# Moving the compressed branch and four out-branch tiles in a fused three-block transformer kernel

## What is computed

```python
blocks = t[:, :, cmp_idx] + pos_emb                    # 15 windows of 32 tokens, keys and values
k_cmp = rms_norm(jax.nn.gelu(flat_k @ w1[0]) @ w2[0], k_gain[0])
v_cmp = jax.nn.gelu(flat_v @ w1[1]) @ w2[1]
sc = jnp.einsum('bgrqd,bgcd->bgrqc', qb, k_cmp) * SCALE
pc = masked_softmax(sc, cmp_end[None, :] <= t[:, None])
o_cmp = jnp.einsum('bgrqc,bgcd->bgrqd', pc, v_cmp)
...
o = gates[0] * o_cmp + gates[1] * o_slc + gates[2] * o_win
y = (o * jax.nn.silu(z)) @ w_out
```

## Time and profile before

| | us |
|---|---|
| runs of the kernel before, median of 3 | 863.43 (860.35 to 863.61) |
| the profiled execution's own time | 864.82 |
| its span, first to last instruction | 863.0 |
| TensorE busy in the span | 810.6 (94%) |
| VectorE busy | 551.3 (64%) |
| ScalarE busy | 420.1 (49%) |
| mean granted TensorE clock | 0.982 of full |

### The profile page before, as it was taken

One profiled execution on the slowest core, in us unless ns is written; L12 is line 12 of the kernel. 1 busy time (PEld: TensorE's weight loads), 2 busy tenths in 40 slices (PEclk: granted clock), 3 DMA queues, 4 the chain that ended last, 5 costly groups with the idle time before them and its releaser, 6 DMA issues.

```text
span 863.0 us, 13766 instructions
## 1 busy us (share of the span) xinstructions
PE 810.6 (94%) x5402; PEld 716.2 (83%) x5402; DVE 551.3 (64%) x930; ACT 420.1 (49%) x820; POOL 114.0 (13%) x114
## 2 busy tenths in 40 slices
PE   4989798998979899999999999998999999999997
PEld 3768797776869687999988988888997788999995
DVE  5897667846796946345635657676675646555555
ACT  5434636844646634446436445553444434444443
POOL 2334004521522402000000000011000000000000
PEclk9989899999999999999999999998999999999999
DMA  8746310213533234553532433333544646655541
GB/s 310 205 155 196 99 49 2 98 68 117 185 104 126 71 123 146 165 178 126 166 101 89 157 118 127 99 114 119 183 154 140 198 144 223 203 187 194 189 154 49
DMA packets 93504, 121.42 MB, mean 141 GB/s; under 512 B 8760, under 2 KB 69616, under 8 KB 93440
## 3 DMA queue, kind: packets, MB, share of 16 engines
q1 hardware_dynamic: 92432, 117.80, 42.1%
q0 software_dynamic: 432, 1.57, 0.5%
q10 hardware_dynamic: 576, 1.17, 0.4%
HBM read 119.48 MB, written 1.05 MB: 140 GB/s over the span
## 4 chain that ended last, share of the span: by engine, by line
PE 77%; DVE 13%; issue 3%; ACT 2%; POOL 1%; POOLq 0%; DVEq 0%; ACTq 0%
PE bank L411 21%; PE bank L413 21%; PE bank L412 21%; DVE w_lo L1443 3%; PE bank L547 1%; DVE small L1534 1%; PE bank L603 1%; PE bank L919 1%; PE bank L418 1%; PE bank L417 1%; PE bank L561 1%; PE bank L541 1%; DVE h_lo L1568 1%; DVE xres L1646 1%; PE bank L859 1%
## 5 line engine op out<-in xcount | busy, mean ns | idle before, releaser
L1443 DVE TENSOR_TENSOR w_lo<-raw,w_hi 128x1024 fp32r<-128x1024 f32 x216 | 268.4, 1248 | 142.3 <-ACT w_hi L1053 140.2
L1053 ACT CAST w_hi<-raw 128x1024 fp32r<-128x1024 f32 (+1 forms) x217 | 226.0, 1045 | 201.0 <-PE bank L413 179.2
L411 PE MATMUL bank<-h_hi,w_hi 128*128 128x256 f32 (+1 forms) x800 | 230.4, 288 | 4.0 <-DVE w_lo L1443 2.9
L412 PE MATMUL bank<-h_lo,w_hi 128*128 128x256 f32 (+1 forms) x800 | 227.3, 284 | 0.0
L413 PE MATMUL bank<-h_hi,w_lo 128*128 128x256 f32 (+1 forms) x800 | 226.4, 283 | 0.0
L411 PEld LDWEIGHTS bank<-h_hi,w_hi 128*128 128x128 f32 x800 | 151.3, 189 | 9.5 <-issue 6.7
L413 PEld LDWEIGHTS bank<-h_hi,w_lo 128*128 128x128 f32 x800 | 152.1, 190 | 0.0
L412 PEld LDWEIGHTS bank<-h_lo,w_hi 128*128 128x128 f32 x800 | 151.7, 190 | 0.4
L411 PE MATMUL bank<-w_hi,h_hi 128*128 128x512 f32 (+1 forms) x288 | 115.8, 402 | 11.9 <-DVE w_lo L1443 6.2
L413 PE MATMUL bank<-w_hi,h_lo 128*128 128x512 f32 (+1 forms) x288 | 113.0, 392 | 0.0
L412 PE MATMUL bank<-w_lo,h_hi 128*128 128x512 f32 (+1 forms) x288 | 113.0, 392 | 0.0
(11 more groups left out here) (309 smaller groups left out, 1234.5 us busy)
## 6 DMA issues: line engine op xcount, KB each, us to landing
raw<-in_w_in SPq DMA_DIRECT2D x24, 1024.0 KB, 5.1
raw<-in_a_w_in SPq DMA_DIRECT2D x14, 1024.0 KB, 5.5
raw<-in_w_ffn_gate SPq DMA_DIRECT2D x11, 1024.0 KB, 5.3
raw<-in_w_ffn_up SPq DMA_DIRECT2D x11, 1024.0 KB, 5.4
raw<-in_w_ffn_down SPq DMA_DIRECT2D x11, 1024.0 KB, 4.9
raw<-in_b_w_in SPq DMA_DIRECT2D x9, 1024.0 KB, 5.2
raw<-in_w_gate SPq DMA_DIRECT2D x8, 1024.0 KB, 5.3
raw<-in_a_w_out SPq DMA_DIRECT2D x4, 1024.0 KB, 5.2
```

The costliest lines, as they stand in the source:

```text
L411: mm(o, lh, rh, start=start, stop=False)
L412: mm(o, lh, rl, start=False, stop=False)
L1053: nc.scalar.copy(split(w_hi, s), rawsub(s)[0]).then_inc(S["hi_ready"], 1)
L1443: V.tensor_tensor(split(w_lo, s), rawsub(s)[0], split(w_hi, s).bitcast(F), ALU.subtract).then_inc(S["lo_ready"], 1)
```

## The change

Five edits. In the first block, the transposes of the compressed inputs (0 to 3) go to banks 0 to 3 and stand between the panels `a_s` and `a_w`; ScalarE's copies of them follow its work on `a_s`; the query and key transposes are spread between the z tiles, and the compression matmuls follow z tile 0. The 32 score matmuls, four at a time, alternate with the eight steps of z tile 5. In the differential attention, branch tiles 0 to 3 of `br_sb` go into rounds 8 and 9, and VectorE's and ScalarE's order follows. The third output projection waits for six merged tiles, not eight, before its first half, and for all eight before its second. The sum of the two statistics goes from GpSimd to VectorE for the first token tile of each norm and for both tiles of the last norm.

```diff
--- before.py
+++ after.py
@@ -498,12 +498,10 @@
                 for e, src in enumerate(srcs, e0):
-                    if phase == 0 and 4 <= e < 8:
-                        pe.wait_ge(S["tq_c"], e - 3)
-                    elif e >= 4:
+                    if e >= (4 if phase else 8):
...
                     for j, t in enumerate(src):
-                        last = nc.tensor.transpose(tbank(e)[:, P * j:P * j + P], t, ident)
+                        last = nc.tensor.transpose((ps[e] if phase == 0 and e < 4 else tbank(e))[:, P * j:P * j + P], t, ident)
@@ -630,6 +628,8 @@
                         pe.wait_ge(S[ready], base + step * (q + 1))
+                    elif n == 3:
+                        pe.wait_ge(S["y_df"], 8)
@@ -669,9 +669,12 @@
             pe.wait_ge(S["rp_act"], 6)
+            pe.wait_ge(S["rp_c"], 2)
+            head_transposes(0, 0, k_tiles(0, 4) + k_tiles(1, 4))
...
             weights_ready(s)
+            pe.wait_ge(S["tq_c"], 4)
@@ -682,33 +685,27 @@
             za = first["a_z"]
+            pe.wait_ge(S["rp_free"], 8)
+            pe.wait_ge(S["rp_act"], 8)
+            pe.wait_ge(S["rp_out"], 4)
+            head_transposes(4, 0, q_tiles(0))
...
             o.then_inc(S["gl_ps"], 1)
-            z_tiles(0, za, 1, 2)
-            pe.wait_ge(S["rp_free"], 8)
-            pe.wait_ge(S["rp_act"], 8)
-            pe.wait_ge(S["rp_c"], 2)
-            head_transposes(0, 0, k_tiles(0, 4))
-            pe.wait_ge(S["rp_free"], 10)
-            pe.wait_ge(S["rp_out"], 4)
-            head_transposes(2, 0, k_tiles(1, 4) + q_tiles(0) + q_tiles(1))
-            pe.wait_ge(S["gates"], 1)
-            pe.wait_ge(S["tq_c"], 4)
...
             last.then_inc(S["cm_ps"], 1)
+            pe.wait_ge(S["rp_free"], 10)
+            head_transposes(6, 0, q_tiles(1))
+            z_tiles(0, za, 1, 2)
+            pe.wait_ge(S["rp_out"], 6)
+            head_transposes(8, 0, k_tiles(2, 4))
             z_tiles(0, za, 2, 3)
-            pe.wait_ge(S["rp_out"], 8)
-            head_transposes(8, 0, k_tiles(2, 4) + k_tiles(3, 4))
-            z_tiles(0, za, 3, 4)
@@ -716,16 +713,29 @@
             last.then_inc(S["cm_ps2"], 1)
-            z_tiles(0, za, 4, 5)
+            pe.wait_ge(S["rp_out"], 8)
+            head_transposes(10, 0, k_tiles(3, 4))
+            z_tiles(0, za, 3, 4)
...
             nc.tensor.transpose(ps[3][:, 256:320], kcd, ident[0:64, 0:64]).then_inc(S["cm_ps3"], 1)
-            z_tiles(0, za, 5, 6)
+            z_tiles(0, za, 4, 5)
             pe.wait_ge(S["cm_kt"], 1)
-            for qt in range(2):
-                for h in range(NH):
+            def compressed_scores(a, b):
+                for i in range(a, b):
+                    qt, h = divmod(i, NH)
...
                               kc[:, h // 4].rearrange("p i c -> p (i c)"), start=True, stop=True)
-            last.then_inc(S["cm_s"], 1)
+                return last
+            pe.wait_ge(S["z_free"], 4)
+            weights_ready(za + 5)
+            wh, wl = split(w_hi, za + 5), split(w_lo, za + 5)
+            for kt in range(KT):
+                last = three(ps[1][:, 0:T], wh[:, kt, :], wl[:, kt, :], tok(0, kt), tok(1, kt), kt == 0, kt == KT - 1)
+                scored = compressed_scores(4 * kt, 4 * kt + 4)
+            last.then_inc(S["sub_used"], 1)
+            scored.then_inc(S["cm_s"], 1)
@@ -942,6 +952,15 @@
+            def br_sb_tile(f):
+                if f < 2:
+                    pe.wait_ge(S["gt_t"], 15 + f)
+                elif f < 4:
+                    pe.wait_ge(S["d_p"], 13 + f)
+                else:
+                    pe.wait_ge(S["y_sb"], f - 3)
+                fm_tile(first["br_sb"] + f, om(o1_hi), om(o1_lo), ps[f % 4][:, 0:T])
@@ -951,11 +970,15 @@
                     pe.wait_ge(S["zb_olo"], 8)
+                if h >= 8:
+                    br_sb_tile(2 * h - 16)
...
                     gate_tile(2 * h + 1)
+                else:
+                    br_sb_tile(2 * h - 15)
@@ -968,12 +991,9 @@
-            pe.wait_ge(S["gt_t"], 16)
-            for f in range(8):
-                if f >= 4:
-                    pe.wait_ge(S["y_sb"], f - 3)
-                fm_tile(first["br_sb"] + f, om(o1_hi), om(o1_lo), ps[f % 4][:, 0:T])
-                if f == 4:
+            for f in range(4, 8):
+                br_sb_tile(f)
+                if f == 5:
@@ -982,7 +1002,7 @@
                 fm_tile(first["br_df"] + f, om(o2_hi), om(o2_lo), ps[f % 4][:, 0:T])
-            pe.wait_ge(S["y_df"], 8)
+            pe.wait_ge(S["y_df"], 6)
@@ -1098,7 +1118,7 @@
                 act.wait_ge(S["tq_ps"], e + 1)
-                b = tbank(e)[:, :].rearrange("p (g n) -> p g n", g=4)
+                b = ps[e][:, :].rearrange("p (g n) -> p g n", g=4)
@@ -1197,25 +1217,33 @@
                     head_item(first[n] + 4, b, 256, vv[j][:, i, :], ps[b][:, 256:512], 0, 4 + 2 * j + i)
+                if n == "a_s":
+                    for i in range(4):
+                        c_copy(i, i // 2, i % 2)
...
             za = first["a_z"]
-            split_hi_to(za + 5)
+            for i in range(2):
+                q_hi(4 + i, 0, 0, i)
+            split_hi_to(za + 4)
...
             A(sm[:, 48:144], sm[:, 48:144], ACT.Tanh, scale=0.5).then_inc(S["gl_t"], 1)
-            split_hi_to(za + 6)
-            z_tanh(0, za, 1)
-            for i in range(4):
-                c_copy(i, i // 2, i % 2)
-            for i in range(4):
-                q_hi(4 + i, 0, i // 2, i % 2)
+            split_hi_to(za + 5)
+            q_hi(6, 0, 1, 0)
...
             A(xg, xg, ACT.Tanh, scale=0.7978845608028654).then_inc(S["cm_t"], 1)
-            for i in range(4):
-                key_hi(8 + i, 0, i // 2, i % 2, 4)
-            for f in range(2, 6):
+            q_hi(7, 0, 1, 1)
+            z_tanh(0, za, 1)
+            split_hi_to(za + 6)
+            for i in range(2):
+                key_hi(8 + i, 0, 0, i, 4)
+            z_tanh(0, za, 2)
+            split_hi_to(za + 7)
+            for i in range(2):
+                key_hi(10 + i, 0, 1, i, 4)
+            for f in range(3, 6):
@@ -1371,8 +1399,8 @@
                     df_squares(h - 3)
-            split_hi_to(first["br_sb"] + RING - 1)
             for h in range(5, 8):
+                split_hi_to(first["br_sb"] + h - 5 + RING)
@@ -1452,9 +1480,12 @@
+                c = 2 * n + tt
+                if tt == 0:
+                    dve.wait_ge(S["n_sq"], 4 * n + 2)
+                    V.tensor_scalar(st_var[:, c:c + 1], st_ss[:, n, 0, 0:1], st_ss[:, n, 0, 1:2], EPS, ALU.add, ALU.add).then_inc(S["n_ss"], 1)
...
                 dve.wait_ge(S["n_rstd"], 2 * n + tt + 1)
-                c = 2 * n + tt
@@ -1743,7 +1774,8 @@
             za = first["a_z"]
-            split_lo_to(za + 5)
+            for i in range(2):
+                q_lo(4 + i, 0, i, 0, i)
@@ -1751,47 +1783,49 @@
             z_gate(0, 0)
-            split_lo_to(za + 6)
+            split_lo_to(za + 4)
...
             V.tensor_scalar(sm[:, 48:144], sm[:, 48:144], 0.5, 0.5, ALU.mult, ALU.add).then_inc(S["gates"], 1)
-            dve.wait_ge(S["gates"], 1)
-            z_gate(0, 1)
-            for i in range(4):
-                q_lo(4 + i, 0, i, i // 2, i % 2)
+            split_lo_to(za + 5)
...
             V.tensor_tensor(xg, xg, xh, ALU.mult).then_inc(S["cm_x"], 1)
-            for i in range(4):
-                key_lo(8 + i, 4 + i, i // 2, i % 2, 4)
+            q_lo(6, 0, 2, 1, 0)
...
             V.scalar_tensor_tensor(out=hidT[:, :, 0:CMP], in0=xg, scalar=1.0, in1=xh, op0=ALU.add, op1=ALU.mult).then_inc(S["cm_hid"], 1)
+            q_lo(7, 0, 3, 1, 1)
...
             V.tensor_copy(vrep, bc(hidT[64:P], [64, 4, 4, 16], 2)).then_inc(S["cm_hid"], 1)
-            split_lo_to(za + 7)
-            z_gate(0, 2)
+            z_gate(0, 1)
+            split_lo_to(za + 6)
+            key_lo(8, 4, 0, 0, 4)
...
             V.tensor_scalar(kss[:, 1:2], kss[:, 0:1], 1.0 / HD, EPS, ALU.mult, ALU.add).then_inc(S["cm_var"], 1)
+            key_lo(9, 5, 0, 1, 4)
+            z_gate(0, 2)
+            dve.wait_ge(S["cm_rstd"], 1)
+            link(V.tensor_scalar(k2, k2, kss[:, 2:3], None, ALU.mult))
+            V.tensor_tensor(kcd.rearrange("p (u d) -> p u d", u=2), bc(k2, [64, 2, HD], 1), bc(gb[0:64, 1, :], [64, 2, HD], 1), ALU.mult).then_inc(S["cm_k"], 1)
+            split_lo_to(za + 7)
+            for i in range(2):
+                key_lo(10 + i, 6 + i, 1, i, 4)
+            dve.wait_ge(S["cm_ps3"], 1)
+            kt_ = ps[3][:, 256:320].rearrange("p (g c) -> p g c", g=4)
+            link(V.tensor_copy(kc[:, :, 0], kt_))
+            V.tensor_tensor(kc[:, :, 1], kt_, kc[:, :, 0].bitcast(F), ALU.subtract).then_inc(S["cm_kt"], 1)
...
                                      bc(cst[:, C_BM:C_BM + 8], [P, 8, HD], 2), ALU.mult))
-            dve.wait_ge(S["cm_rstd"], 1)
-            link(V.tensor_scalar(k2, k2, kss[:, 2:3], None, ALU.mult))
```

(37 more changed lines are left out.)

## The result

The changed kernel takes 849.07 us, the median of four runs (848.00 to 850.14), against 863.38 us for the kernel before in the same comparison: a ratio of 0.9839, 95% interval 0.9816 to 0.9862, so 12 to 16 us less. The forecast was 848.0. The profiled execution took 850.14 us with a span of 848.3 us, 14.7 less than the 863.0 of the earlier trace rows.

What follows compares the result with a forecast made beforehand. TensorE, busy 94% of the span, bounds the kernel; only its waits and low-clock stretches offer time. 9.3 + 5.2 + 1.0 + 0.5 = 16.0 off 864.82 gives 848.8, or 847.4 on the median's scale; forecast 848.0, range 844.5 to 853.

Steps and rivals of the forecast that it cites:

- First block: From the end of `a_s` to scores(2): the new order brings scores(2) at 120.6 instead of 129.95, 9.3 us gained.
- the wait before the second matrix: First block: TensorE waits about 1.5 us for VectorE before the second compression matrix, a new wait and an expected sign.
- The compression matmuls: First block: 4.46 us before, nearly all at low clock; between 2.25 and 4.46 at full clock, taken as 3.0.
- The check beside the sum: First block: old waits of 5.8 us plus low-clock losses of 3.4 and 1.7, less new wait and allowance, give 8.9.
- The near misses: First block: VectorE's normed keys and their halves arrive with 0.3 us to spare each; 0.5 us booked.
- The alternating tile: First block, z tile 5 mixed with the 32 scores: 6.35 us at the old rates, 0.79 a step for seven scores.
- Differential tail: Differential attention's end to the second branch: a branch tile before each wait cuts 35.3 us to about 30, 5.2 gained.
- The y_df wait: Third output projection: its first half no longer waits for the last two merged tiles, 1.0 us gained.
- The norm's sums: Norms: sum on VectorE takes some 0.15 us instead of 0.30 on GpSimd; three norms give 0.5, the last 0.
- that rival: The clock falls again in the wait before the second matrix or the alternating tile: 1.7 to 3.4 us, about 850.5; chance 0.15.
- VectorE's queue: Rival: VectorE's queue is longer than summed in the first block or tail, lengthening TensorE's waits; about 852, chance 0.12.
- ScalarE's copies would be late: Rival, first block: ScalarE's copies in front of the z splits make the kernel slower, 864 and more; chance 0.01.

Runs made afterwards that it cites:

- e6_half: The changed kernel with only half of the 64 compression matmuls, leaving out half of the sum over positions; 849.31 us, ratio 0.9830.
- e8_before_warm: The kernel before, order and waits unchanged, with spare identity transposes on TensorE in its longest waits; 859.27 us, ratio 0.9949.
- e5_block: The changed kernel with the 32 compressed score matmuls in one block behind the sixth z tile instead of alternating; 850.20 us, ratio 0.9843.
- e9_block_warm: The changed kernel with the scores in one block and spare identity transposes in its four longest waits outside the first norm; 848.36 us, ratio 0.9826.
- e4: The kernel before with only the norm sums moved to VectorE (first tile of each norm, both of the last); 863.96 us, ratio 1.0005.
- e1: The kernel before with only the compressed branch's part: transposes, copies, compression and scores of the first block; 852.27 us, ratio 0.9871.
- e3: The kernel before with only the split wait for merged tiles before the third output projection; 861.52 us, ratio 0.9984.
- e2: The kernel before with only the differential tail's part: branch tiles in the head loop, with their splits and gatings; 858.57 us, ratio 0.9948.

## Why the prediction was right

The time, 848.0 for 849.07, and the sum by parts stand:

- **First block, 9.3 forecast, 9.6 measured.** Right as a sum, with two terms off that cancel, and one of the forecast's signs, the wait before the second matrix, not seen. The compression matmuls, booked at 3.0 us ("nearer to the low end"), took 4.44 (86.22 to 90.66), the high end of the bounds: 69 ns for each of 64 at full clock, as at low clock in the earlier trace rows. The new wait of 1.5 us before the second matrix did not come, because TensorE was that much later: VectorE was done at 98.12, in forecast time 99.2 against 98.95. e6_half shows the other side of the same sum: shorten the compression, and the wait is there, 2.07 us. So this error could not move the time. The check beside the sum agreed (8.9) by luck: it priced the low stretch at 94 to 102 at 3.4 us, and e8_before_warm, which takes that stretch away, gains 0.46.
- **The near misses**, 0.5 booked, cost nothing; VectorE met each key step. The second matrix began some 0.2 us later than forecast, so that 0.3 of the 0.5 was left as the block's gain over forecast.
- **The alternating tile**: steps of 0.80 us (106.39, 107.19), so 6.4 us as booked from the earlier trace rows (0.79 a step). The Trainium skill's rule (TensorE: Matmul & The Clock Gate, LDWEIGHTS), by which seven loads would bound the step at an estimated 0.75 us, isn't met: the order of narrow and wide matmuls saved nothing by itself. What alternating bought, the forecast did not price apart: the traces of e5_block and e9_block_warm put it at 1.5 and 3.1 us, by keeping the clock up; in an execution in which the clock holds behind the block, as in e4's trace, it buys none of that.
- **Differential tail, 5.2 forecast, 5.3 measured**, 30.0 us for the stretch as summed; the 0.5 us wait for the gating of tile 0 did not show. The forecast booked 3.4 us of clock here; what it did not say is that the old code has this fall in some executions and not in others (e1, 114.35 us). That the profile from which the forecast was made had it was luck.
- **The y_df wait**, 1.0 forecast, 1.1 in e3's trace (its median can't tell 1 us from none). **The norm's sums**, 0.5: the waits for `h_lo` went from 5.1 to 4.9 in all, and in the second to fourth norm from 1.30, 1.30 and 1.39 to 1.15, 1.16 and 1.24, that is 0.15 each, while the first, 1.09 and 1.38, varies from 0.9 to 1.4 with the edit or without. The last norm, booked at 0, cost 0.5 (7.29 against 6.79 us). The forecast had ScalarE's last statistic 0.3 late, which it is (0.25), and the second tile's sum saving as much. That saved 0.14 (1.13 us from the statistic to ScalarE's scaling, against 1.27), with GpSimd's power at 0.71 us where it was 0.56, and the transfers took the rest. So the term of 0.5 was in the net about 0.
- **Rivals.** The clock did fall in the changed kernel, but not where that rival put it (the wait before the second matrix, the alternating tile). It fell in places that the change doesn't touch, at 240 and 290 us, and cost there with the wait at 238 about 2.5 us, the size that the rival had. The early part of the program gave 1.07 us by a shorter fall at 58 to 63, so that the time came out near the forecast in part by luck. VectorE's queue was as long as summed. That ScalarE's copies would be late was not seen.

What stays open is what decides whether a given wait brings a fall. The same waits in the tail had it in the kernel before and not in e1. That the falls at 240 and 290 came with the order of the new code isn't shown: e1, e5_block and e6_half had none at 290.

## What to carry to other kernels

Where two engines run level (here TensorE and VectorE at the second compression matrix), price them together: an error on one comes back as a wait of the other, and speeding up one of them buys nothing. A wait's price is its length plus, in some executions, the low clock behind it, and where the matmuls run no slower at the low clock (the compression here), or another engine bounds the stretch (the second block's z tiles, 15.54 and 15.53 us), that second part is free. Look in several executions before a low stretch is booked as gain. And look at each place to which a small edit goes: the same sum, moved between engines, saved 0.15 us at three norms and cost 0.5 at the last. Spread narrow matmuls between wide ones, or put spare transposes in a long wait whose bank is free: here the fillers took 1.1 us (846.86 against 847.96) off the best order and made all its runs alike.

## What the runs showed of the hardware

- 64 matmul instructions of 64 loaded columns and 75 moving ones take 4.4 to 4.5 us at a granted clock of 1.00 and near 0.5 alike.
- A block of 32 narrow matmuls (3.5 us, TensorE busy by the profile throughout, at full clock) was followed by the low clock (0.50) in the traces of the kernel before, e2, e3, e5_block, e8_before_warm and e9_block_warm, in e5_block and e9_block_warm with no wait in the 20 us ahead of it; in e4_norm's it was not.
- The low clock costs nothing where another engine sets the pace: the second block's z tiles took 15.54 us with a fall from 241 to 245 us and 15.53 with none.
- The same add of two 128x1 columns before the last power: moved from GpSimd to VectorE, it made the end of the span 0.5 us longer in eight traces against five.
- Nearly all scatter of this kernel is the clock: the kernel before had 860.3 us at a mean granted clock of 0.988 and 865.5 at 0.980 in one comparison; with the fillers all nine runs of the changed kernel were within 0.2 us at 0.997 to 0.999.
